# Another order of the odd latent heads' work on ScalarE and VectorE, and of the opening pair of the neighbourhood attention

## What is computed

```
q_lat, kv_lat, k_pe, g_mla, na_q, na_k, na_v, g_na = split(rmsnorm(h) @ w_in)
# latent attention: 8 heads, 128 + 64 wide, all 528 keys, queries in 4 tiles of 128
q = rmsnorm(q_lat) @ w_uq ; k, v = rmsnorm(kv_lat) @ w_ukv ; each normed, rotary part turned
p = softmax((q_nope @ k_nope.T + q_pe @ k_pe.T) * scale) ; y_mla = (p @ v) * silu(g_mla)
# neighbourhood attention: 16 heads of 64, in pairs; a window of keys and a bias table
p = softmax(q @ k_win.T * scale + bias | q @ k_meta.T * scale + meta_bias)
y_na = (p @ v) * silu(g_na)
h = h + concat(y_mla, y_na) @ w_out
```

## Time and profile before

| | us |
|---|---|
| median of 3 runs | 1265.69 |
| lowest, highest | 1264.14, 1265.83 |
| the profiled execution | 1265.12 |
| its span, first to last instruction | 1263.4 |
| mean granted clock of TensorE | 0.997 of full |

### The profile page before, as it was taken

One profiled execution on the slowest core, in us unless ns is written; L12 is line 12 of the kernel. 1 busy time (PEld: TensorE's weight loads), 2 busy tenths in 40 slices (PEclk: granted clock), 3 DMA queues, 4 the chain that ended last, 5 costly groups with the idle time before them and its releaser, 6 DMA issues.

```text
span 1263.4 us, 20098 instructions
## 1 busy us (share of the span) xinstructions
PE 1245.8 (99%) x6808; PEld 1034.9 (82%) x6808; DVE 744.4 (59%) x1407; ACT 475.4 (38%) x1039; POOL 641.1 (51%) x427
## 2 busy tenths in 40 slices
PE   8999999999999999999999999999999999999998
PEld 8877777877788888888887878888988788888876
DVE  5867655566955454452234788888744566666640
ACT  4343333412422222221112466666501455555531
POOL 5543333248354434445554155544437877777722
PEclk8999999999999999999999999999999999999999
DMA  7332222233232332323334211111134332222213
GB/s 208 100 79 72 84 66 84 61 90 101 84 116 83 100 99 88 95 80 101 95 95 114 67 50 51 50 34 48 52 82 113 84 93 80 79 79 79 66 34 100
DMA packets 190899, 105.42 MB, mean 83 GB/s; under 512 B 19206, under 2 KB 186476, under 8 KB 190844
## 3 DMA queue, kind: packets, MB, share of 16 engines
q1 hardware_dynamic: 190180, 103.61, 29.0%
q0 software_dynamic: 432, 0.69, 0.2%
q10 hardware_dynamic: 232, 0.40, 0.1%
HBM read 102.57 MB, written 2.10 MB: 83 GB/s over the span
## 4 chain that ended last, share of the span: by engine, by line
PE 90%; DVE 3%; ACT 2%; POOL 2%; issue 1%; DMA 1%; SPq 0%; DVEq 0%; ACTq 0%; POOLq 0%
PE ps L397 20%; PE ps L398 20%; PE ps L399 20%; PE ps L428 8%; PE ps L1621 1%; PE ps L1623 1%; PE ps L1622 1%; PE ps L908 1%; PE ps L1538 1%; PE ps L1570 1%; PE ps L1279 1%; DMA w_raw<-in_w_in_dram 1%; POOL w_low L376 1%; PE ps L1550 1%; PE ps L410 1%
## 5 line engine op out<-in xcount | busy, mean ns | idle before, releaser
L376 POOL TENSOR_TENSOR w_low<-w_raw,w_high 128x1024 fp32r<-128x1024 f32 x180 | 440.2, 2448 | 438.8 <-DVE w_high L371 434.3
L397 PE MATMUL ps<-h_high,w_high 128*128 128x512 f32 x752 | 302.6, 402 | 1.2 <-DVE ng L2895 1.0
L398 PE MATMUL ps<-h_low,w_high 128*128 128x512 f32 x752 | 297.3, 395 | 0.0
L399 PE MATMUL ps<-h_high,w_low 128*128 128x512 f32 x752 | 296.0, 394 | 0.0
L371 DVE CAST w_high<-w_raw 128x1024 fp32r<-128x1024 f32 x183 | 145.8, 798 | 92.2 <-DMA w_raw<-in_w_down_dram 33.9
L397 PEld LDWEIGHTS ps<-h_high,w_high 128*128 128x128 f32 x752 | 141.3, 188 | 34.1 <-issue 2.3
L399 PEld LDWEIGHTS ps<-h_high,w_low 128*128 128x128 f32 x752 | 141.5, 188 | 32.3
L398 PEld LDWEIGHTS ps<-h_low,w_high 128*128 128x128 f32 x752 | 141.3, 188 | 29.8 <-issue 1.0
L1901 ACT ACTIVATE z<-ps,cv 128x512 f32<-128x512 f32 x42 | 32.7, 778 | 148.3 <-PE ps L399 148.3
L2542 DVE SCALAR_TENSOR_TENSOR z<-ps,cv,z 128x511 f32<-128x511 f32 x42 | 31.5, 749 | 92.7 <-ACT z L1901 92.7
L398 PE MATMUL ps<-m_low,w_high 128*128 128x512 f32 x176 | 69.4, 395 | 0.0
(11 more groups left out here) (408 smaller groups left out, 2571.5 us busy)
## 6 DMA issues: line engine op xcount, KB each, us to landing
w_raw<-in_w_in_dram SPq DMA_DIRECT2D x150, 256.0 KB, 3.3
w_raw<-in_w_up_dram SPq DMA_DIRECT2D x88, 256.0 KB, 3.2
w_raw<-in_w_out_dram SPq DMA_DIRECT2D x44, 256.0 KB, 3.0
w_raw<-in_w_down_dram SPq DMA_DIRECT2D x32, 256.0 KB, 3.0
w_raw<-in_w_down_dram SPq DMA_DIRECT2D x16, 192.0 KB, 2.6
rel<-in_rel_bias_dram SPq DMA_DIRECT2D x16, 192.0 KB, 3.6
w_raw<-in_w_ob_dram SPq DMA_DIRECT2D x8, 256.0 KB, 2.9
w_raw<-in_w_oa_dram SPq DMA_DIRECT2D x8, 256.0 KB, 4.1
```

What stands on the lines that cost most here:

```text
L376: pool.tensor_tensor(w_low[:, n % RING, :], w_raw[:, n % RAW, :], w_high[:, n % RING, :].bitcast(F32), ALU.subtract).then_inc(low_made, 1)
L397: pe.matmul(acc, wh, mh, start=first and k == 0, stop=False)
L398: pe.matmul(acc, wh, ml, start=False, stop=False)
L399: done = pe.matmul(acc, wl, mh, start=False, stop=last and k == tiles - 1)
```

## The change

On ACT, in `head_then_odd`: the exponent of tile 1 goes ahead of the copy of tile 0, that of tile 2 between the roots of the keys and of the queries, and that of tile 3 behind the rounding of the queries, which now waits for the scores of tile 3. On DVE, in the same body: the scaling of tile 1 goes ahead of the rest of tile 0, and the maximum of tile 2 ahead of a weight rounding and the norming of the keys. On PE, once: the third part of head 0's gate goes ahead of the turning of `k_pe`. In the opening neighbour pair only: DVE makes the gate ahead of the rounding of the strip N_NA + 7 instead of behind it; ACT squares the next keys between the first two exponents instead of behind them; POOL makes the four large table sums of the second head ahead of the keys' squares' low part and the two small ones where all six stood. No operation is added or taken away.

```diff
--- before.py
+++ after.py
@@ -793,7 +793,7 @@
             for n in range(N_OM + 4, N_OM + 6):
                 make_low(pool, n)
 
-            def bias_table(i, c, hs=(0, 1), meta=True):
+            def bias_table(i, c, hs=(0, 1), meta=True, parts=(0, 6)):
 
                 pool.wait_ge(s["rel_in"], i * 64 + (32 * c + 32))
                 if c:
@@ -804,7 +804,7 @@
                     for o, m, r, n in ((NA_OFF[1] + META, 8, 8, 2), (NA_OFF[1] + META + P, P + 8, P + 8, 2),
                                        (END + META, 3 * P + 8, P + 8, 2),
                                        (NA_OFF[3], 5 * P + 8, 8, 2), (META, 3 * P, P, 1),
-                                       (NA_OFF[3] + P + META, 5 * P + P + 8, P + 8, 1)):
+                                       (NA_OFF[3] + P + META, 5 * P + P + 8, P + 8, 1))[parts[0]:parts[1]]:
                         to = nb[:, z_, h, o:o + n * HALF_TILE]
                         if n > 1:
                             to = to.rearrange("p (b c r) -> p b c r", c=8, r=8)
@@ -840,10 +840,12 @@
                     ahead = N_NA + 4 * (c + 2)
                     if c:
                         bias_table(i, c + 1)
+                    else:
+                        bias_table(i, 1, (1,), False, (0, 4))
                     squares_low(i, c + 1, 0)
                     make_low(pool, ahead, i * 8)
                     if c == 0:
-                        bias_table(i, 1, (1,), False)
+                        bias_table(i, 1, (1,), False, (4, 6))
                 if c:
                     y_parts(i, c - 1)
                 if more:
@@ -1497,9 +1499,9 @@
             kpe_sums()
             m_sums(0, 0, 1)
             m_sums(0, 0, 2)
+            m_gate(0, 0, 2)
             kpe_turn()
             m_project(0, 0, 2)
-            m_gate(0, 0, 2)
             m_gate(0, 0, 3)
             m_turn_v(0, 0)
             pe.wait_ge(low_made, N_MLA + 3)
@@ -2082,17 +2084,18 @@
                 m_square_high(i, c + 1)
                 if c:
                     y_rounded(i, c - 1)
+                m_expo(i, c, 1)
                 m_copy(i, c, 0)
-                m_expo(i, c, 1)
                 m_root(i, c + 1, 1)
+                m_expo(i, c, 2)
                 m_root(i, c + 1, 2)
                 m_high_of(i, c + 1, 0)
                 m_copy(i, c, 1)
-                m_expo(i, c, 2)
                 m_high_of(i, c + 1, 1)
                 m_keep_v(i, c + 1)
+                act.wait_ge(s["s_scored"], i * 8 + (4 * c + 4))
+                m_high_of(i, c + 1, 2)
                 m_expo(i, c, 3)
-                m_high_of(i, c + 1, 2)
                 m_copy(i, c, 2)
                 m_place_v(i, c + 1)
 
@@ -2226,9 +2229,11 @@
 
             def pair(i, c):
                 expo(i, c, 0)
+                if c == 0:
+                    square(i, c + 1, 0)
                 expo(i, c, 1)
-                square(i, c + 1, 0)
                 if c:
+                    square(i, c + 1, 0)
                     y_rounded(i, c - 1)
                 copy_a(i, c, 0)
                 root_ln(i, c + 1, 0)
@@ -2744,11 +2749,11 @@
                     m_gated(i, c - 1, 1)
                     m_gate(i, c)
                 m_top(i, c, 1)
+                m_scale(i, c, 1)
                 m_rest(i, c, 0)
-                m_scale(i, c, 1)
+                m_top(i, c, 2)
                 make_high(dve, ahead, i * 4)
                 m_normed(i, c + 1, 1)
-                m_top(i, c, 2)
                 m_rest(i, c, 1)
                 m_scale(i, c, 2)
                 m_normed(i, c + 1, 2)
@@ -2896,8 +2901,8 @@
 
             def pair(i, c):
                 ahead = N_NA + 4 * (c + 2)
-                gate(i, c)
                 if c:
+                    gate(i, c)
                     gated(i, c - 1, 1)
                 masked(i, c, 0)
                 masked(i, c, 1)
@@ -2945,6 +2950,7 @@
             normed(0, 0, 1)
             make_high(dve, N_NA + 5)
             make_high(dve, N_NA + 6)
+            gate(0, 0)
             make_high(dve, N_NA + 7)
             pair(0, 0)
             with dve.Fori(0, 3) as i:
```

## The result

| | before | after |
|---|---|---|
| median, us | 1265.28 (4 runs, 1264.14 to 1265.83) | 1272.46 (4 runs, 1272.14 to 1272.64) |
| ratio of after to before, 95% interval | | 1.0058 (1.0046 to 1.0070) |
| the profiled execution, us | 1265.12 | 1272.32 |
| its span, us | 1263.4 | 1270.6 |

The change makes the kernel 7.2 us slower. The forecast was slower by 3.6, 1269.3, in a range that ends at 1272.0: the sign and the place are right, the size is half of what was measured.

A forecast was written before the change was run, and what follows sets the result against it. TensorE, busy 99% of the span, was taken as the bound, so only its waits count. Loop +6.1, head 0 -1.4, gate -0.4, neighbour pair -0.6 give +3.7, 1268.8 us, or 1269.3 as median; range 1265.0 to 1272.0.

The forecast's parts named there:

- Part 1: Odd body in the latent loop: late copy(1) delays `mp_low`, TensorE waits 2.0 us at weigh(0), three times, +6.1 us.
- A second statement of part 1: Loop, VectorE: tile 2's maximum waits for TensorE's scores, so moving it up in the queue brings nothing; it ends at 843.54.
- Parts 2 and 3: Head 0: old waits 2.6 us go, new ones 1.1 to 1.2 come, -1.4; gate ahead of keys' turn covers `k_pe` wait, -0.4.
- Part 4: Opening neighbour pair: `ng` wait goes, first `y_low` 0.4 us later, second `y_low` wait of 1.05 goes; -0.6 us.
- The wait of about 2 us named as a sign for the first sum: Opening neighbour pair: TensorE's wait for the first `y_low`, line 1600, would be about 2 us long.
- the step on `y_low`: Opening pair: four large table sums, 2.8 us on GpSimd behind its weight part, start the first `y_low` 0.4 us later.
- The first (the late copy is hidden): Rival, loop: the late copy is covered and the change does what it says, 1263.3 us; chance 0.13.
- the second (openings in full): Rival: openings win 6.0 us in full while the loop pays 6.1, 1265.8 us, no change; chance 0.14.
- The third: Rival, loop: GpSimd holds VectorE's queries' scaling and tile 2's probabilities, each turn costs 1 us more, 1272.3 us; chance 0.10.
- The chance for slower, 0.69: Whole kernel: chance of a time from 1268.2 us up, 0.59 from the forecast and 0.10 from a rival.

The follow-up runs named there:

- experiment 2: Changed kernel with 15 filler matmuls of 256 columns in TensorE's wait ahead of the weighing in heads 2, 4 and 6; 1269.29 us.
- experiment 3: Changed kernel with ScalarE's copy of tile 1 ahead of the third exponent again in heads 2, 4 and 6; 1267.95 us.
- experiment 6: Changed kernel, heads 2, 4, 6: ScalarE's copy(1) ahead of the third exponent, VectorE's maximum of tile 2 behind the keys' norming, both as before; 1264.94 us.
- experiment 5: Changed kernel with VectorE's order of before in heads 2, 4 and 6, ScalarE's new order kept; 1273.35 us.
- experiments 7 and 8: Changed kernel, old loop order; opening pair's table sums: all six behind weight part (7, 1262.38 us), or four large behind first `y_low`, ahead of weight part (8, 1262.45).
- experiment 1: Changed kernel with ScalarE's and VectorE's order of before in heads 2, 4 and 6, new order only in head 0 and the openings; 1262.9 us.

## Why the prediction was wrong in size and right in mechanism

**Part 1, the loop: mechanism and size of the wait right, its price short.** Predicted 2.0 us a turn at line 1297, for `mp_low`, three times; it is 1.94 to 1.95, and copy(1) came 0.53 behind the keys' rounding as worked out. The step that failed is "2.0 us of new wait, three times: +6.1", which priced the wait at its own length. TensorE then ran at half its clock behind two of the three waits, 3.1 us more in the profiled execution; experiment 2 shows it, since with the same late start and TensorE kept busy the kernel is 3.2 us faster. With this term the sum is +3.7 + 3.1 = 6.8. The other 0.4 is the loop's waits, which come to 6.5 by the shift and not 6.1: the weighing starts 2.08 later a turn and not 2.03, and its second matmul another 0.1 later. The 0.15 at turn(1), which the prediction put at nothing, only makes the wait behind it shorter, as it said. The errors of the openings (-1.6 for -1.8 and -0.9 for -0.6) and the 0.1 between loop and pair cancel. The prediction gave no chance to a change of the clock: the kernel before had waits of 1.0 and 1.1 us in both openings and full clock there, and the prediction did not ask whether that holds at 2 us, a length that no row of that kernel's loop shows.

**A second statement of part 1 was wrong without harming the sum.** That the earlier maximum of tile 2 "brings nothing" was right, but it isn't free: it holds the keys' norming behind a wait for TensorE. With copy(1) back ahead of the third exponent 1.28 us a turn stay (experiment 3), 0.9 of it from the maximum (experiment 6). In the changed kernel this was hidden behind ScalarE's larger delay (experiment 5). I had followed the queue of ScalarE behind the moved instruction, and of VectorE only the moved instruction itself. I named what is queued behind the new waits for expo(2), not for the maximum.

**Parts 2 and 3, head 0 and the gate.** Predicted -1.4 and -0.4. The shift of the matmuls gives -1.5 for head 0 and -0.1 for the gate: the wait for `k_pe` is gone and TensorE was 0.85 ahead, but 0.75 of it (0.5 by the row) came back at `kpe_low`, where I had counted 0.2. The three new waits of head 0 were named with their places (turn(1) 0.5, weighing 0.3, last transposition 0.3); the rows show 0.5, 0.2 and 0.4.

**Part 4, the opening pair.** Predicted -0.6, from a first sum 0.4 late and 1.05 won at the second; the shift is -0.9. It is +8.1 both ahead of the pair and at its first sum, so TensorE was level there and not 0.4 behind, and the second wait gave 0.9. The wait of about 2 us named as a sign for the first sum came as 0.6 for the probabilities and 1.1 for `y_low` (both by the row). GpSimd, then VectorE, after; these rows answer to the earlier trace rows:

```profile
997.28 2.40 POOL L376 TENSOR_TENSOR w_low<-w_raw,w_high 128x1024 fp32r<-128x1024 f32 x1
...
999.65 2.58 POOL L813 TENSOR_TENSOR nb<-rel,mask 128x128 f32<-128x128 f32 x4
...
1002.18 1.36 POOL L823 TENSOR_TENSOR y_low<-sq,y_high 128x528 fp32r<-128x528 f32 x1
...
1008.42 1.29 POOL L823 TENSOR_TENSOR y_low<-sq,y_high 128x512 fp32r<-128x512 f32 x1
```

```profile
998.84 1.60 DVE L2855 TENSOR_SCALAR ne<-ne,nm 128x224 f32<-128x224 f32 x2
```

The four large sums stand between the weight part and the low part and end at 1002.2, as the step said: 2.5 us, where 2.8 was taken. VectorE's two scalings of the probabilities from 998.84 took 1.60 together, where the same two took 0.58 in the kernel before: GpSimd was at the weight part until 999.68 and then at the sums, where it had been through with the weight part before they began. TensorE's transposition waited 0.6 for the pair of them. In experiments 7 and 8, where GpSimd was through with its weight part 0.3 us after they began and no sums followed, they took 0.69. But TensorE waited 0.6 for them there as well, so the wait for the probabilities can't be put down to the overlap alone. Experiments 7 and 8 confirm the step on `y_low`: with the low part ahead of the sums its wait is gone.

**The rivals.** The first (the late copy is hidden) and the second (openings in full) are out: experiment 1 gives what the openings bring, 1.9. The third forecast nearly the time measured, 1272.3, but by a mechanism that isn't there: no wait at turn(2) of tile 2's probabilities in the loop. That its number comes so near is luck. The chance for slower, 0.69, was on the side that came.

## What to carry to other kernels

Price a new wait of TensorE at more than its length: behind 1.9 us the granted clock halved in two of three cases, which cost 1.5 us more each time, while 1.3 us and less left it alone in every profile here. When a step moves up in an in-order queue, follow everything that now stands behind it, above all what another engine needs soon: here a copy of 0.6 us, put behind an exponent and a root, kept TensorE waiting for 2 us. And ask of a body that runs in several places where its old waits were: it was worth reordering in head 0, which had them, and cost in the loop, which had none.

## What the runs showed of the hardware

- Granted clock 0.50 for 3.3 us behind waits of 1.94 us (twice of three times) and 2.28 us (twice of three, beginning 0.9 and 0.7 us after TensorE had gone on), 1.00 behind all waits of 1.28 and of 1.0 us. No run here shows why waits of one length had either outcome. Where 15 matmuls of 256 columns filled the wait it stayed at 1.00. The Trainium skill, page "TensorE: Matmul & The Clock Gate", Part 1, says that the array's clock falls to half after idleness and comes back with activity; the trace agrees.
- At half clock 256-column matmuls start 0.21 us apart, against 0.12.
- The scaling of 128 x 512 on VectorE takes 0.49 us in the median of its 32 runs after. In the second turn (849.54) it took 1.13 and ended 0.28 after GpSimd's operation of 1.30 from 849.09; in head 0 of the kernel before it took 1.99 and ended 0.28 after GpSimd's weight part. The same delay both times: it ends when GpSimd's operation has been over for 0.28. The Trainium skill, page "SBUF — State Buffer", section "SBUF: two separate sides", says that VectorE and GpSimd share a pair of ports which one of them holds for a whole instruction; the trace agrees.
